# One place a turn for score items and conditioning rows, and two bank pairs for the channel tiles

## The chip, the cores and the metric

The kernel runs on one core of a Trainium2 chip. What is measured is the device time of one execution, in microseconds (us); smaller is better.

## What is computed

One layer of a decoder for 512 prompt tokens and 8 x 8 sample tokens, 576 in all, 1024 wide. The part that matters here is the first half of the layer:

```
mod = silu(c) @ w_ada + b_ada            # 6 x 1024 columns, 9 conditioning vectors
sh1, sc1, g1, sh2, sc2, g2 = split(mod, 6)
h = rmsnorm(x, norm_pre1) * (1 + sc1) + sh1
bg, cg, ua, q, k, v, r, lr, ga, gb = split(h @ w_in)
y_a = bg * causal_conv3(cg * ua)         # branch A, 1024 channels
scores = q k^T with decay, causal        # branch B, 4 heads, evaluated in blocks
merged = sigmoid(ga) * y_a + sigmoid(gb) * y_b
```

All inputs are float32. The large products are made of three passes over high and low parts (`hi*hi`, `hi*lo`, `lo*hi`).

## The kernel before

The program is written by hand as five instruction streams (TensorE, VectorE, ScalarE, GpSimd, SyncE) that wait for each other's semaphores. Each stream runs strictly in the order of its code.

The convolution stage is the loop `for j in range(KT)` in each stream, with eight turns, one for each 128 channels. In a turn TensorE makes four **channel tiles** with `channel_tile` (L1874): `cg`, `ua`, `bg` and `ga`, called tile 0 to tile 3 below. Each is 48 matmuls of 128x128 by 288 tokens into one pair of PSUM banks; there are four pairs, banks 0-1, 2-3, 4-5 and 6-7. Before the change the tiles go round the pairs 0, 1 and 2, so a tile waits until the one three tiles back has been taken out of PSUM. Who takes them out:

- tile 0: ScalarE copies it to `buf_a` (`cg_done`, L1024);
- tile 1: VectorE multiplies it by `buf_a` into `ext` (`u_done`, L1373, three pieces), then convolves `ext` (L519, L522);
- tile 2: VectorE multiplies it by the convolution (`t_done`, L1389);
- tile 3: ScalarE takes its sigmoid into `buf_b` (`sga_done`, L1042), and VectorE multiplies `y_a` by it (`ya_done`).

Three kinds of small work ride along on TensorE, all of them with a stationary operand only 32 columns wide:

- **Score items** (`score_item`, L1982). Turn j does level j of the block scores: five items in turn 0, three in turns 1 to 3, two in turns 4 to 7. Each is written to bank 7 and merged into `score` by VectorE (`take_item`, L581). Since all items share bank 7, each waits until the one before has been taken (`item_taken`).
- **Conditioning rows** (`ada_pair`, L2009). Two a turn, 4 matmuls of 512 columns each, into bank 6. The two together are one group of sums. VectorE copies them to `rows_ada` (L1411).
- **The way back** (`mod_back`, L1995). It turns the rows of the turn before round into bank 7, from where `take_mod` (L586) adds them to `mod`.

Where they stand is set by the variable `e` in TensorE's loop: even `e` is a channel tile, then come the items that `after_tile(j, e)` names; `ada_pair` stands at `e` = 3 and 7, `mod_back` at `e` = 6.

```
slots = (0, 2, 4, 6, 7) if j == 0 else (0, 2, 4)
```

On the other streams: ScalarE splits the weights (`high`, L931), GpSimd makes their low halves (`low`, L860), SyncE issues the loads in one fixed order (L667 for tiles, L680 for conditioning weights). The load of conditioning weights x waits for `ada_mm >= (x - 4) // 2 + 1`, and all loads behind it wait too. `qd_exp(j + 1)` on ScalarE waits until all items of level j have been made.

Of the kernel before, what the change touches and what calls it, by code (L numbers as in the profile page):

```python
# [39 lines left out]
KT = D // P  # L40
# [80 lines left out]
def layer_program(nc, a):  # L121
# [127 lines left out]
    def one_bank(b):  # L249
        return bank[b // 2][:, b % 2, :]  # L250
# [7 lines left out]
    def S(name):  # L258

        if name not in sems:  # L260
            sems[name] = nc.alloc_semaphore(name)
        return sems[name]
# [18 lines left out]
    def kc(tile):  # L281

        return tile[:, :].rearrange("p (k c) -> p k c", c=P)
# [31 lines left out]

    def c1_pair(j, i):

        return (4 * j + i) % 3

    ada_raw = [raw_c[i] for i in (0, 1, 4, 5)]  # L320

# [95 lines left out]
        items += [(lv, g) for g in ([[0], [1], [2], [3]] if B == 0 else [[0, 1], [2, 3]])]  # L417
        items += [(lv, [4])] if B < 8 else []

    def after_tile(j, e):  # L420

        level = [i for i, it in enumerate(items) if it[0] == j]
        slots = (0, 2, 4, 6, 7) if j == 0 else (0, 2, 4)
        return [i for i, slot in zip(level, slots) if slot == e]

    def items_to(lv):

        return sum(1 for it in items if it[0] <= lv)
# [135 lines left out]
    def take_item(dve, i):  # L564

        lv, chunks = items[i]
        B = LEVELS[lv]
        src = one_bank(7)
        ch, nch = chunks[0] * HEADS, len(chunks) * HEADS
        m = ROWS[chunks[0]]  # L570
        dve.wait_ge(S("item"), i + 1)
        if B == 0:
            dst = score[0:m, ch:ch + nch, 0:m]
            msk = ident[0:m, 0:m].bitcast(I32).rearrange("p (o t) -> p o t", o=1).to_broadcast([m, nch, m])
            data = src[0:m, 0:nch * m].rearrange("p (c t) -> p c t", t=m)
        else:
            dst = score[0:m, ch:ch + nch, 0:m].rearrange("p c (n s b) -> p c n s b", s=2, b=B)[:, :, :, 1, :]
            msk = mask[0:m, lv - 1, 0:m // 2].bitcast(I32).rearrange("p (o n b) -> p o n b", o=1, b=B) \
                .to_broadcast([m, nch, m // 2 // B, B])
            data = src[0:m, 0:nch * m // 2].rearrange("p (c n b) -> p c n b", c=nch, b=B)  # L580
        dve.copy_predicated(dst, msk, data).then_inc(S("item_taken"), 1)  # L581

    def take_mod(dve, j):
# [68 lines left out]
    with nc.Block() as block:  # L652
# [609 lines left out]
        def _(dve):  # L1262
# [96 lines left out]

            for j in range(KT):  # L1360
                n = TILE_C1 + 4 * j
                for i in after_tile(j, 0):
                    take_item(dve, i)

                if j > 0:
                    dve.wait_ge(S("tail_done"), 2 * j)
                    dve.wait_ge(S("conv"), 3 * j)
                hist = ext[:, S0E:EXT].rearrange("p (s w) -> p s w", w=TS + 2)[:, :, 0:2]
                dve.tensor_copy(hist, mix0[:, :, j].rearrange("p (s w) -> p s w", w=2)).then_inc(S("hist"), 1)
                dve.wait_ge(S("cg_done"), j + 1)  # L1370
                dve.wait_ge(S("ring_free"), n + 2)
                for src, dst, lo, hi in conv_pieces(c1_pair(j, 1), ext, 2, TS + 2, 2):
                    dve.tensor_tensor(dst, src, piece(buf_a, lo, hi), ALU.mult).then_inc(S("u_done"), 1)  # L1373
                for i in after_tile(j, 2):
                    take_item(dve, i)
                dve.wait_ge(S("u_done"), 3 * (j + 1))
                dve.wait_ge(S("hist"), j + 1)
                if j > 0:
                    dve.wait_ge(S("t_done"), 3 * j)
                conv(dve, ext, cv, [prm[:, CW + 8 * w + j:CW + 8 * w + j + 1] for w in range(3)],  # L1380
                     prm[:, CB + j:CB + j + 1], "conv", 3 * j)
                tails(dve, tail_mix[:, :, j], "tail_done")
                for i in after_tile(j, 4):
                    take_item(dve, i)
                dve.wait_ge(S("conv"), 3 * j + 3)

                dve.wait_ge(S("ring_free"), n + 3)
                for src, cvp, lo, hi in conv_pieces(c1_pair(j, 2), cv, 0, TS + 2, 2):
                    dve.tensor_tensor(piece(y_a[:, j, :], lo, hi), src, cvp, ALU.mult).then_inc(S("t_done"), 1)  # L1389
                if j + 1 < KT:  # L1390
                    dve_level(dve, j + 1)
                else:

                    dve.wait_ge(S("exps"), 1)
                    dve.tensor_tensor(k[:, :, :], k[:, :, :], suf[:, :, :], ALU.mult).then_inc(S("decayed"), 1)
                    dve.wait_ge(S("exps"), 2)
                    dve.tensor_tensor(q[:, :, :], q[:, :, :], pre[:, :, :], ALU.mult).then_inc(S("decayed"), 1)
                for i in after_tile(j, 6):
                    take_item(dve, i)
                if j > 0:  # L1400
                    take_mod(dve, j - 1)
                dve.wait_ge(S("t_done"), 3 * (j + 1))
                dve.wait_ge(S("sga_done"), j + 1)
                dve.tensor_tensor(y_a[:, j, :], y_a[:, j, :], buf_b[:, :], ALU.mult).then_inc(S("ya_done"), 1)
                for i in after_tile(j, 7):
                    take_item(dve, i)

                dve.wait_ge(S("ada_mm"), 2 * (j + 1))
                if j > 0:
                    dve.wait_ge(S("back"), j)  # L1410
                dve.tensor_copy(rows_ada[:, :], one_bank(6)[:, :]).then_inc(S("rows_ada"), 1)  # L1411

            take_mod(dve, KT - 1)
            dve.wait_ge(S("mod_done"), 9)
# [360 lines left out]
        def _(pe):  # L1775
# [176 lines left out]
            def score_item(i):  # L1952

                lv, chunks = items[i]
                B = LEVELS[lv]
                dst = one_bank(7)
                if B:
                    pe.wait_ge(S("qd_done"), lv)
                    if B > 1:
                        pe.wait_ge(S("kd_done"), lv - 1)  # L1960

                if i > 0:
                    pe.wait_ge(S("item_taken"), i)
                if lv >= 2:
                    pe.wait_ge(S("mod_done"), lv)
                kk = kd if B > 1 else k
                col = 0
                for c in chunks:
                    w = ROWS[c]
                    for h in range(HEADS):  # L1970
                        wide = max(B, 16) if B else 32
                        for g in range(w // 32):
                            key = 32 * g
                            if B == 0:
                                at_, rhs = key, q[:, h, P * c:P * c + w]
                            else:
                                if key % (2 * B) >= B > 16:
                                    continue
                                at_ = key // (2 * B) * B if B > 16 else key // 2
                                first = (h * T + P * c) // 2 if B < 8 else (h * SEQ + P * c) // 2  # L1980
                                rhs = qd[:, first:first + w // 2]
                            ins = pe.matmul(dst[key:key + 32, col + at_:col + at_ + wide],  # L1982
                                            kk[:, h, P * c + key:P * c + key + 32], rhs[:, at_:at_ + wide], start=True, stop=True)
                        col += w // 2 if B else w
                ins.then_inc(S("item"), 1)

            def mod_back(j):

                pe.wait_ge(S("rows_ada"), j + 1)
                pe.wait_ge(S("item_taken"), items_to(min(j + 1, KT - 1)))  # L1990
                if j > 0:
                    pe.wait_ge(S("mod_done"), j + 1)
                for m in range(4):
# [18 lines left out]

            pe.wait_ge(S("c_split"), 5)
            for j in range(KT):
                for e in range(8):
                    if e % 2 == 0:
                        n = TILE_C1 + 4 * j + e // 2
                        pe.wait_ge(S("w_lo_done"), n + 1)
                        if n < TILE_C1 + 2:
                            pe.wait_ge(S("v_summed"), n - TILE_C1 + 1)  # L2020
                        before = 4 * j + e // 2 - 3
                        if before >= 0:
                            name, count = (("cg_done", 1), ("u_done", 3), ("t_done", 3), ("sga_done", 1))[before % 4]
                            pe.wait_ge(S(name), count * (before // 4 + 1))
                        channel_tile(kc(w_hi[n % 4]), kc(w_lo[n % 4]), c1_pair(j, e // 2), (h_hi, h_lo))
                    elif e % 4 == 3:
                        ada_pair(2 * j + e // 4)
                    for i in after_tile(j, e):
                        score_item(i)
                    if e == 6 and j > 0:  # L2030
                        mod_back(j - 1)

            def tails_and_mod():

# [312 lines left out]
```

## Time and profile before

| | |
|---|---|
| median of 3 runs | 1012.21 us (1010.62 to 1012.27) |
| span of the profiled execution, first to last instruction | 1007.4 us |
| what lies around that span, against the median | 4.8 us |
| TensorE matmuls busy | 987.9 us, 98% of the span |
| VectorE, ScalarE, GpSimd busy | 543.0, 385.9, 228.6 us |

Busy time is the union of an engine's instructions. Matmuls overlap in their pipeline, so a busy TensorE can still do little work: how far apart two matmuls start says more than how long one lasts.

### The profile page before, as it was taken

The page shows a single profiled execution, that of the slowest core. Times are in us where ns is not written, and L with a number is a line of the kernel's source. Part 1 is how long each engine was busy: PE and PEld are TensorE (multiplying, and loading weights), DVE is VectorE, ACT ScalarE, POOL GpSimd, SP SyncE. Part 2 cuts the span into 40 slices and gives each one's busy share as a digit, 9 for nine tenths or more (in the row PEclk, how much of TensorE's full clock was granted, in tenths as well). Part 3 has the DMA queues.
Part 4 walks back from the last instruction along what each step waited for, and adds up shares of the span by engine and source line. Part 5 has one row for each costly group of instructions (what it writes and reads, how often), then busy time and mean ns, then how long its engine had stood idle before and what let it go on. Part 6 is the DMA issues. An engine that isn't in the chain of part 4 may idle for free.

```text
span 1007.4 us, 18705 instructions
## 1 busy us (share of the span) xinstructions
PE 987.9 (98%) x7743; PEld 897.7 (89%) x7743; DVE 543.0 (54%) x868; ACT 385.9 (38%) x588; POOL 228.6 (23%) x124
## 2 busy tenths in 40 slices
PE   7799999999999999999999999999999999999997
PEld 5689889999999999899998789999999999888886
DVE  2501104667555665346436688877777778750204
ACT  4532533143343334443463345333333334533212
POOL 2043433233343333233343020000000000013330
PEclk9999999999999999999999999999999999999999
DMA  9565344598366657545427042222322222323212
GB/s 354 171 93 180 116 90 96 129 115 136 106 193 165 138 128 139 91 105 160 123 91 219 1 124 86 64 85 84 85 84 85 84 85 63 126 64 100 79 59 94
DMA packets 144132, 115.59 MB, mean 115 GB/s; under 512 B 11353, under 2 KB 123761, under 8 KB 143025
## 3 DMA queue, kind: packets, MB, share of 16 engines
q1 hardware_dynamic: 143953, 114.38, 43.5%
q8 instruction: 61, 1.00, 0.4%
q14 instruction: 22, 0.18, 0.1%
q10 hardware_dynamic: 96, 0.04, 0.0%
HBM read 107.02 MB, written 7.35 MB: 114 GB/s over the span
## 4 chain that ended last, share of the span: by engine, by line
PE 93%; SPq 2%; DMA 1%; ACT 1%; DVE 1%; issue 1%; DVEq 0%
PE pair L1874 50%; PE pair L1929 16%; PE pair L2250 10%; PE pair L2203 5%; PE pair L2009 1%; PE pair L1982 1%; DMA raw<-in_w_in 1%; PE pair L1861 1%; SPq L667 1%; SPq L705 1%; PE pair L1921 1%; PE pair L2072 1%; PE pair L2061 1%; PE pair L1922 1%; PE pair L1923 1%
## 5 line engine op out<-in xcount | busy, mean ns | idle before, releaser
L1874 PE MATMUL pair<-h_hi,w_hi 128*128 128x288 f32 x1280 | 285.6, 301 | 0.1
L1874 PE MATMUL pair<-h_hi,w_lo 128*128 128x288 f32 x1280 | 279.1, 296 | 0.0
L1874 PE MATMUL pair<-h_lo,w_hi 128*128 128x288 f32 x1280 | 278.8, 295 | 0.0
L860 POOL TENSOR_TENSOR w_lo<-raw,w_hi 128x1024 fp32r<-128x1024 f32 x57 | 140.1, 2459 | 601.5 <-ACT w_hi L931 601.5
L1874 PEld LDWEIGHTS pair<-h_hi,w_hi 128*128 128x128 f32 x1280 | 207.2, 189 | 18.4 <-issue 16.3
L1874 PEld LDWEIGHTS pair<-h_lo,w_hi 128*128 128x128 f32 x1280 | 207.6, 188 | 0.0
L1874 PEld LDWEIGHTS pair<-h_hi,w_lo 128*128 128x128 f32 x1280 | 207.7, 188 | 0.0
L931 ACT ACTIVATE w_hi<-raw 128x1024 fp32r<-128x1024 f32 x70 | 73.5, 1056 | 160.5 <-PE pair L1923 75.7
L860 POOL TENSOR_TENSOR w_lo<-raw_c,w_hi 128x1024 fp32r<-128x1024 f32 x24 | 68.2, 2846 | 124.7 <-ACT w_hi L931 124.7
L1929 PE MATMUL pair<-w_hi,f_hi 128*128 128x512 f32 x176 | 68.9, 391 | 0.0
L1929 PE MATMUL pair<-w_lo,f_hi 128*128 128x512 f32 x176 | 68.7, 390 | 0.0
L1929 PE MATMUL pair<-w_hi,f_lo 128*128 128x512 f32 x176 | 68.5, 389 | 0.0
L1164 ACT ACTIVATE cv<-cv 128x592 f32<-128x592 f32 x22 | 15.4, 700 | 106.3 <-DVE cv L522 106.3
L2250 PE MATMUL pair<-t_hi,w_hi 128*128 128x288 f32 x144 | 42.5, 295 | 0.0
L2250 PE MATMUL pair<-t_lo,w_hi 128*128 128x288 f32 x144 | 42.5, 295 | 0.0
L2250 PE MATMUL pair<-t_hi,w_lo 128*128 128x288 f32 x144 | 42.4, 295 | 0.0
L1929 PEld LDWEIGHTS pair<-w_hi,f_lo 128*128 128x128 f32 x176 | 33.1, 188 | 7.0
L1929 PEld LDWEIGHTS pair<-w_hi,f_hi 128*128 128x128 f32 x176 | 33.0, 188 | 7.0
L1929 PEld LDWEIGHTS pair<-w_lo,f_hi 128*128 128x128 f32 x176 | 33.0, 188 | 6.8
L522 DVE SCALAR_TENSOR_TENSOR cv<-ext,ffp,cv 128x592 f32<-128x592 f32 x44 | 36.7, 834 | 1.6
L931 ACT ACTIVATE w_hi<-raw_c 128x1024 fp32r<-128x1024 f32 x24 | 25.2, 1055 | 26.8 <-PE pair L1874 12.0
L2250 PE MATMUL pair<-h_hi,w_hi 128*128 128x288 f32 x108 | 31.8, 294 | 0.0
(349 smaller groups left out, 1603.5 us busy)
## 6 DMA issues: line engine op xcount, KB each, us to landing
raw<-in_w_in SPq DMA_DIRECT2D x256, 64.0 KB, 3.1
raw_c<-in_w_ada SPq DMA_DIRECT2D x32, 512.0 KB, 5.8
raw_c<-in_w_in SPq DMA_DIRECT2D x192, 64.0 KB, 3.6
raw<-in_w_up SPq DMA_DIRECT2D x24, 512.0 KB, 4.7
raw<-in_w_down SPq DMA_DIRECT2D x22, 512.0 KB, 3.7
raw_up<-in_w_up SPq DMA_DIRECT2D x20, 512.0 KB, 3.8
ada_first<-in_w_ada SPq DMA_DIRECT2D x8, 1024.0 KB, 13.8
raw<-in_w_in SPq DMA_DIRECT2D x8, 512.0 KB, 4.7
```

The costliest lines, as they stand in the source:

```text
L522: dve.scalar_tensor_tensor(dst[:, :], src[:, tap:tap + CONV], w[tap], dst[:, :], ALU.mult, ALU.add) \
L667: sp.dma_start(dst[:, i, :], src[:, i, :]).then_inc(S(raw_name(n)), 16)
L705: sp.dma_start(ada_first[:, i, :], w_ada[P * i:P * i + P, 0:2 * D]).then_inc(S(f"ada_in{i}"), 16)
L860: pool.tensor_tensor(lo, raw_tile(n)[:, :], hi.bitcast(F32), ALU.subtract).then_inc(S("w_lo_done"), 1)
L931: act.activation(dst, raw_tile(n)[:, :], ACT.Copy).then_inc(S("w_hi_done"), 1)
L1164: act.activation(cv[:, :], cv[:, :], ACT.Gelu_apprx_tanh).then_inc(S("gelu_done"), 1)
L1861: ins = pe.matmul(bank[n][:, half, 0:HALF], w[:, i, :], x[:, i, HALF * half:HALF * half + HALF], start=i == 0 and p == 0, stop=i == KT - 1 ...
L1874: ins = pe.matmul(bank[pair][:, half, 0:HALF], w[:, i, :], x[:, i, HALF * half:HALF * half + HALF], start=i == 0 and p == 0, stop=i == KT ...
L1921: pe.matmul(dst[0:64, :], first_i[:, 0:64], wl[:, 0, :], start=False, stop=False)
L1929: ins = pe.matmul(one_bank(banks[t])[0:m, :], x, w[:, i, :], start=first and i == 0 and p == 0, stop=last and i == 1 and p == 2)
L2203: ins = pe.matmul(bank[wo_pair(x)][0:n, c, :], xx, w[:, 512 * c:512 * c + 512], start=y == 0 and p == 0, stop=y == KT - 1 and p == len(pas ...
L2250: ins = pe.matmul(dst, w[:, i, :], x[:, i, :], start=i == 0 and p == 0, stop=i == 3 and p == 2)
```

## The change

Every score item of a turn stands behind tile 1, and so do the way back and both conditioning pairs. Only turn 0 puts its last two items behind tile 3, since there are five. The items go to three banks (4, 5 and 7) in place of one; in bank 7 they stand at column 64, clear of the 36 columns of the way back. To free banks 4 and 5, the channel tiles alternate between pairs 0 and 1, so each now waits for the tile two back. VectorE takes the items after the tails of the convolution and copies `rows_ada` before the `t_done` products.

```
     def c1_pair(j, i):
-        return (4 * j + i) % 3
+        return (4 * j + i) % 2
...
-    def after_tile(j, e):
-        level = [i for i, it in enumerate(items) if it[0] == j]
-        slots = (0, 2, 4, 6, 7) if j == 0 else (0, 2, 4)
-        return [i for i, slot in zip(level, slots) if slot == e]
+    def after_tile(j, i):
+        level = [x for x, it in enumerate(items) if it[0] == j]
+        return level[:3] if i == 1 else level[3:] if i == 3 else []
+    def item_place(x):
+        lv = items[x][0]
+        slot = x - items_to(lv - 1)
+        return one_bank((4, 5, 7, 4, 5)[slot]), 64 if slot == 2 and lv > 0 else 0
...
                 tails(dve, tail_mix[:, :, j], "tail_done")
-                for i in after_tile(j, 4):
+                for i in after_tile(j, 1):
                     take_item(dve, i)
+                if j > 0:
+                    take_mod(dve, j - 1)
+                dve.wait_ge(S("ada_mm"), 2 * (j + 1))
+                if j > 0:
+                    dve.wait_ge(S("back"), j)
+                dve.tensor_copy(rows_ada[:, :], one_bank(6)[:, :]).then_inc(S("rows_ada"), 1)
                 dve.wait_ge(S("conv"), 3 * j + 3)
...
-                if i > 0:
-                    pe.wait_ge(S("item_taken"), i)
-                if lv >= 2:
-                    pe.wait_ge(S("mod_done"), lv)
+                if lv > 0:
+                    pe.wait_ge(S("item_taken"), items_to(lv - 1))
+                elif i > 2:
+                    pe.wait_ge(S("item_taken"), i - 2)
...
-                pe.wait_ge(S("item_taken"), items_to(min(j + 1, KT - 1)))
+                pe.wait_ge(S("item_taken"), items_to(j))
...
             for j in range(KT):
-                for e in range(8):
+                for i in range(4):
...
-                        before = 4 * j + e // 2 - 3
+                    before = 4 * j + i - 2
...
+                    if i == 1 and j > 0:
                         mod_back(j - 1)
+                    for x in after_tile(j, i):
+                        score_item(x)
+                    if i == 1:
+                        ada_pair(2 * j)
+                        ada_pair(2 * j + 1)
```

On TensorE, turn 1, the end of tile 1 and what follows it before the change (`raw_c_80` to `raw_c_85` are the four buffers of conditioning weights):

```order
L1982 MATMUL pair<-qd,k 32x16 [waits item_taken,qd_done]
L1982 MATMUL pair<-qd,k 32x16 x31
L2009 MATMUL pair<-raw_c_80,c_wide 32x512 [waits rows_ada,ada_raw_in1,ada_raw_in0]
```

The same place after the change (lines move by three: L1992 is the way back, L1979 a score item, L2006 a conditioning pair):

```order
L1992 MATMUL pair<-fold_all,rows_ada 32x9 [waits item_taken,rows_ada]
L1992 MATMUL pair<-fold_all,rows_ada 32x9 x15
L1979 MATMUL pair<-qd,k 32x16 [waits item_taken,qd_done]
L1979 MATMUL pair<-qd,k 32x16 x31
L1979 MATMUL pair<-qd,k 32x16 [waits item_taken,qd_done]
L1979 MATMUL pair<-qd,k 32x16 x31
L1979 MATMUL pair<-qd,k 32x16 [waits item_taken,qd_done]
L1979 MATMUL pair<-qd,k 32x16 x7
L2006 MATMUL pair<-raw_c_80,c_wide 32x512 [waits rows_ada,ada_raw_in1,ada_raw_in0]
L2006 MATMUL pair<-raw_c_80,c_wide 32x512
L2006 MATMUL pair<-raw_c_81,c_wide 32x512 x2
L2006 MATMUL pair<-raw_c_84,c_wide 32x512 [waits ada_raw_in3,ada_raw_in2]
```

One item and one pair became the way back, three items and both pairs. Behind tiles 0, 2 and 3 nothing small is left in this turn.

On VectorE, turn 1, from the products of tile 1 to those of tile 2, before:

```order
L1373 TENSOR_TENSOR ext<-pair,buf_a 128x8x8
L581 COPY_PREDICATED score<-mask,pair 128x512 [waits item]
L519 TENSOR_SCALAR cv<-ext,prm 128x592 [waits t_done,hist,u_done]
L522 SCALAR_TENSOR_TENSOR cv<-ext,prm,cv 128x592 [waits conv] x2
L527 COPY tail_mix<-ext 128x2
L529 COPY tail_mix<-ext 128x16
L581 COPY_PREDICATED score<-mask,pair 64x4x32 [waits item]
L1389 TENSOR_TENSOR y_a<-pair,cv 128x288 [waits ring_free,conv]
```

And after, with L586 as the taking of an item and L1391 as the copy to `rows_ada`:

```order
L1376 TENSOR_TENSOR ext<-pair,buf_a 128x8x8
L524 TENSOR_SCALAR cv<-ext,prm 128x592 [waits t_done,hist,u_done]
L527 SCALAR_TENSOR_TENSOR cv<-ext,prm,cv 128x592 [waits conv] x2
L532 COPY tail_mix<-ext 128x2
L534 COPY tail_mix<-ext 128x16
L586 COPY_PREDICATED score<-mask,pair 128x512 [waits item] x2
L586 COPY_PREDICATED score<-mask,pair 64x4x32 [waits item]
L591 TENSOR_TENSOR mod<-pair,prm 128x36 [waits back]
L1391 COPY rows_ada<-pair 128x512 [waits back,ada_mm]
L1396 TENSOR_TENSOR y_a<-pair,cv 128x288 [waits ring_free,conv]
```

Three items, the sum into `mod` and the copy to `rows_ada` now stand between the convolution and the products of tile 2.

## Rows read from the trace of the kernel before

**Rows 1.** Cores: span, mean granted TensorE clock.
```profile
core 0: 1007.4 us, clock 0.999
```

**Rows 2.** Chain that ended last, 140 to 420 us: start us, us, what.
```profile
151.59 6.40 PE pair L1874 x48
...
181.53 6.59 PE pair L1874 x48
...
272.36 6.58 PE pair L1874 x48
...
287.79 12.98 PE pair L1874 x96
...
331.70 6.58 PE pair L1874 x48
...
361.23 6.58 PE pair L1874 x48
...
391.53 3.38 PE pair L1874 x24
```

**Rows 3.** Timeline of TensorE, turn 1: start us, us, engine, line, tiles, shapes.
```profile
194.67 0.42 PE L1874 MATMUL pair<-h_lo,w_hi 128*128 128x288 f32 x2
194.93 0.43 PE L1874 MATMUL pair<-h_hi,w_lo 128*128 128x288 f32 x2
195.29 0.73 PE L1982 MATMUL pair<-qd,k 128*32 128x16 f32 x64
195.89 1.06 PE L2009 MATMUL pair<-raw_c,c_wide 128*32 128x512 f32 x8
196.89 0.53 PE L1874 MATMUL pair<-h_hi,w_hi 128*128 128x288 f32 x2
197.26 0.42 PE L1874 MATMUL pair<-h_lo,w_hi 128*128 128x288 f32 x2
...
203.46 0.43 PE L1982 MATMUL pair<-qd,k 128*32 128x16 f32 x16
...
210.40 0.44 PE L1995 MATMUL pair<-fold_all,rows_ada 128*32 128x9 f32 x32
210.68 1.07 PE L2009 MATMUL pair<-raw_c,c_wide 128*32 128x512 f32 x8
211.67 0.53 PE L1874 MATMUL pair<-h_hi,w_hi 128*128 128x288 f32 x2
```

**Rows 4.** Timeline of TensorE: an item of turns 0, 6 and 7.
```profile
179.75 0.46 PE L1982 MATMUL pair<-q,k 128*32 128x32 f32 x32
...
338.21 0.70 PE L1982 MATMUL pair<-qd,kd 128*32 128x32 f32 x32
...
367.74 1.09 PE L1982 MATMUL pair<-qd,kd 128*32 128x64 f32 x32
```

**Rows 5.** All matmuls of `ada_pair` (L2009): duration ns min/median/max, first and last start.
```profile
L2009 PE MATMUL pair<-raw_c,c_wide x128: 589/592/617, 165.2 to 390.9; 128*32 128x512 f32 x128
```

**Rows 6.** Timeline of VectorE, turn 2, from the products of tile 1.
```profile
225.75 0.89 DVE L1373 TENSOR_TENSOR ext<-pair,buf_a 128x288 f32<-128x288 f32 x3 [3.29 <-PE pair L1874]
226.56 1.32 DVE L581 COPY_PREDICATED score<-mask,pair 128x512 f32<-128x512 int32 x1
227.68 1.93 DVE L519 TENSOR_SCALAR cv<-ext,prm 128x592 f32<-128x592 f32 x1
229.64 1.70 DVE L522 SCALAR_TENSOR_TENSOR cv<-ext,prm,cv 128x592 f32<-128x592 f32 x2
```

**Rows 7.** Timeline of ScalarE, end of turn 3; brackets: idle before, releaser.
```profile
271.14 1.06 ACT L931 ACTIVATE w_hi<-raw_c 128x1024 fp32r<-128x1024 f32 x1 [2.39 <-DMA raw_c<-in_w_in]
...
273.51 0.66 ACT L1042 ACTIVATE buf_b<-pair 128x576 f32<-128x576 f32 x1
```

**Rows 8.** Windows of turn 2: us, busy of PE, PEld, DVE, ACT, POOL; PEclk, DMA share, GB/s.
```profile
212.00:242.00 30.00, 29.98 (x384) 27.56 (x382) 21.82 (x23) 10.44 (x10) 11.88 (x5) 1.00 0.99 121
```

**Rows 9.** Waits of SyncE's queue, 150 to 400 us: total us, times, longest.
```profile
SPq L680 <- PE pair L2009: 61.2, 10, 13.8
```

More of the change, by code:

```diff
@@ L567, in take_item @@
         B = LEVELS[lv]
-        src = one_bank(7)
+        src, at_ = item_place(i)
         ch, nch = chunks[0] * HEADS, len(chunks) * HEADS
@@ L574, in take_item @@
             msk = ident[0:m, 0:m].bitcast(I32).rearrange("p (o t) -> p o t", o=1).to_broadcast([m, nch, m])
-            data = src[0:m, 0:nch * m].rearrange("p (c t) -> p c t", t=m)
+            data = src[0:m, at_:at_ + nch * m].rearrange("p (c t) -> p c t", t=m)
         else:
@@ L579, in take_item @@
                 .to_broadcast([m, nch, m // 2 // B, B])
-            data = src[0:m, 0:nch * m // 2].rearrange("p (c n b) -> p c n b", c=nch, b=B)
+            data = src[0:m, at_:at_ + nch * m // 2].rearrange("p (c n b) -> p c n b", c=nch, b=B)
         dve.copy_predicated(dst, msk, data).then_inc(S("item_taken"), 1)
@@ L1361, in _ @@
                 n = TILE_C1 + 4 * j
-                for i in after_tile(j, 0):
-                    take_item(dve, i)
                 if j > 0:
@@ L1373, in _ @@
                     dve.tensor_tensor(dst, src, piece(buf_a, lo, hi), ALU.mult).then_inc(S("u_done"), 1)
-                for i in after_tile(j, 2):
-                    take_item(dve, i)
                 dve.wait_ge(S("u_done"), 3 * (j + 1))
@@ L1397, in _ @@
                     dve.tensor_tensor(q[:, :, :], q[:, :, :], pre[:, :, :], ALU.mult).then_inc(S("decayed"), 1)
[L1398 to L1401, printed above, removed]
                 dve.wait_ge(S("t_done"), 3 * (j + 1))
@@ L1404, in _ @@
                 dve.tensor_tensor(y_a[:, j, :], y_a[:, j, :], buf_b[:, :], ALU.mult).then_inc(S("ya_done"), 1)
-                for i in after_tile(j, 7):
+                for i in after_tile(j, 3):
                     take_item(dve, i)
[L1408 to L1411, printed above, removed]
             take_mod(dve, KT - 1)
@@ L1955, in score_item @@
                 B = LEVELS[lv]
-                dst = one_bank(7)
+                dst, col = item_place(i)
                 if B:
@@ L1960, in score_item @@
                         pe.wait_ge(S("kd_done"), lv - 1)
-                if i > 0:
-                    pe.wait_ge(S("item_taken"), i)
-                if lv >= 2:
-                    pe.wait_ge(S("mod_done"), lv)
+                if lv > 0:
+                    pe.wait_ge(S("item_taken"), items_to(lv - 1))
+                elif i > 2:
+                    pe.wait_ge(S("item_taken"), i - 2)
                 kk = kd if B > 1 else k
-                col = 0
                 for c in chunks:
@@ L2014, in _ @@
             for j in range(KT):
-                for e in range(8):
[L2016 to L2020, printed above, removed]
-                        before = 4 * j + e // 2 - 3
[L2022 to L2030, printed above, removed]
-                        mod_back(j - 1)
+                for i in range(4):
+                    n = TILE_C1 + 4 * j + i
+                    pe.wait_ge(S("w_lo_done"), n + 1)
+                    if n < TILE_C1 + 2:
+                        pe.wait_ge(S("v_summed"), n - TILE_C1 + 1)
+                    before = 4 * j + i - 2
+                    if before >= 0:
+                        name, count = (("cg_done", 1), ("u_done", 3), ("t_done", 3), ("sga_done", 1))[before % 4]
+                        pe.wait_ge(S(name), count * (before // 4 + 1))
+                    channel_tile(kc(w_hi[n % 4]), kc(w_lo[n % 4]), c1_pair(j, i), (h_hi, h_lo))
+                    if i == 1 and j > 0:
+                        mod_back(j - 1)
+                    for x in after_tile(j, i):
[3 more added lines that the diff above has]
+                        ada_pair(2 * j + 1)
             def tails_and_mod():
```

## The prediction

> **What bounds the kernel now.** I read the chain of work that ended last first. From 151.59 us to 391.53 us it consists of TensorE matmuls and nothing else long enough to be listed, turn after turn [rows 2]. So in the convolution stage TensorE sets the time, and what an engine beside it gains or loses counts only if TensorE has to wait for it. The granted clock is 0.999 over the whole span [rows 1] and 1.00 in the stage [rows 8], the higher level of 2.4 GHz, so a matmul costs the same everywhere.
>
> Next I asked how much of the stage is the small work. A channel tile that follows large matmuls takes 6.40 us (the first row of [rows 2]). Where tiles 2 and 3 follow each other the two take 12.98, which is 2 x 6.40 and 0.18 for the small work around them. The stage runs for 391.53 - 151.59 = 239.94 us, and its 32 tiles need 32 x 6.40 = 204.80. The other **35.14 us** are small work and the switches into and out of it. By turns [rows 2]: turn 0 has 29.94 - 25.60 = 4.34, turns 1 to 3 have 90.83 - 76.80 = 14.03, turns 4 and 5 have 59.34 - 51.20 = 8.14, turn 6 has 3.93, turn 7 has 4.70.
>
> Then I took such a place apart with TensorE's timeline [rows 3]. Pairs of large matmuls start 0.26 to 0.27 apart (194.67, 194.93). The first small one starts 0.36 after the last pair: **entering** costs 0.09. The item lasts 0.60 until the conditioning pair starts, and that one 1.00 until the tile starts. The tile's first pair then takes 0.37 (196.89 to 197.26): **leaving** costs 0.10. The largest piece is in the 1.00. A conditioning matmul lasts 0.59 [rows 5] and the eight recorded ones of a pair cover 1.06, so the last starts some 0.48 after the first, and the tile can't start until that last one is nearly through. Since work of the same 32-column shape needn't wait for that (the pair at 195.89 starts while the item's 0.73 still run), the end of a place costs more than its middle. That is what the change can save.
>
> **The change, part by part.**
>
> *Fewer places.* Before, turn 0 has 4 places, turns 1 to 3 have 4 and turns 4 to 7 have 3: 28 in all. After, there is one a turn and a second in turn 0: 9. The matmuls are the same in number and shape, so I price each new place by what stands in it.
>
> - entering 0.09, leaving 0.10 [rows 3];
> - the way back 0.28 until the next small work (210.40 to 210.68);
> - a 64-matmul item 0.60; a 32-matmul item of turn 0 0.28 (its busy 0.46, like the way back's 0.44 [rows 3, 4]); the 16-matmul item 0.15 inside a place, at the 64-matmul item's rate of 9.4 ns, and 0.40 just before a tile (busy 0.43 [rows 3]);
> - an item of turn 6 0.54 and of turn 7 0.93, their busy 0.70 and 1.09 [rows 4] less the 0.16 that overlaps in the way back;
> - the last conditioning pair 1.00 until the tile [rows 3];
> - the first conditioning pair until the second: no row shows it. Eight recorded matmuls on four strips of 32 columns are two rounds. The second round starts before 0.48, so a round is about 0.44 and the pair 0.88. From below it is 0.48, if the second pair's first round starts as soon as the first pair's last matmul has started; from above 1.00, if every pair is waited for as a tile waits. I take 0.88, since no change of shape lies between the two.
>
> Turn 0: 0.09 + 3 x 0.28 + 0.88 + 1.00 + 0.10 = 2.91, and behind tile 3 0.09 + 0.28 + 0.40 + 0.10 = 0.87, together 3.78. Turns 1 to 3: 0.09 + 0.28 + 2 x 0.60 + 0.15 + 0.88 + 1.00 + 0.10 = 3.70 each, 11.10. Turns 4 and 5 without the short item: 3.55 each, 7.10. Turn 6: 3.43. Turn 7: 4.21. The sum is **29.62**, so the stage gets 35.14 - 29.62 = 5.52 shorter, and the first tile behind it loses its 0.10 of leaving: **5.6 us**.
>
> On the second pair the Trainium skill says otherwise. "TensorE: Matmul & The Clock Gate", section "Back-to-back issue gap", gives N/2.4 + 2.5 ns between matmuls at the full clock, 216 ns for 512 columns, where the rows need about 440. With its figure the second pair would cost 0.43 in place of 0.88, and the gain would be an estimated 9.2 us. The trace's own two rounds in 1.06 don't agree with it for these float32 operands.
>
> *Three banks for the items.* The wait of an item for the one before goes. It costs little now, since it lay under other work; I count nothing.
>
> *Two bank pairs for the tiles.* A tile now waits for the one two back, so whoever takes a tile out of PSUM has one tile's time, 6.40 us. Tile 0 of the next turn waits for VectorE's `t_done`. Counted from the end of tile 1, VectorE needs 0.81 for the products, 1.96 and 1.70 for the convolution, at most 3 x 1.12 for the three items [rows 6] and, for two tails, the sum into `mod` and the copy to `rows_ada`, which I bound by one more 1.93: 9.8 us. Tile 2 ends 3.6 + 6.4 = 10.0 us after tile 1, so its products start on time, take about 0.9, and the next turn's tile 0 is 5.5 us further on. What hides the moved work is tile 2 itself. The level work that follows on VectorE moves a little earlier than now, since it doesn't wait for an item behind tile 2. ScalarE's `qd_exp` moves from behind tile 2 to behind tile 1, which is only earlier.
>
> *Loads.* SyncE stands 61.2 us waiting for conditioning pairs [rows 9]. The second pair of a turn now ends some 13 us earlier, so these loads and the tiles' loads behind them are issued earlier. The first pair ends about 2 us later than now behind tile 1 (way back and items stand ahead of it), and one tile's load behind it does too.
>
> **The rivals.**
>
> *ScalarE too late for two pairs.* In turn 3 a high half waited 2.39 us for its transfer, and the sigmoid of tile 3 ended at 274.17 [rows 7]. That tile ended about 1.4 us before turn 4 began at 272.36, at 270.9, so it was 3.2 us late. Before, nobody felt it, since the pair was wanted two tiles later. Now tile 1 of the next turn wants it after 6.4. By then TensorE is ahead by 4.34 + 14.03 - 3.78 - 11.10 = 3.5 us, and if the transfer doesn't come earlier the sigmoid is 6.7 late: a stall of 0.3. With transfers as crowded as in turn 2 (busy share 0.99 at only 121 GB/s [rows 8]) it could be 3 us in one or two turns. Time 1009 or so. For it: that stretch. Against: SyncE issues earlier.
>
> *The transfers set the pace, and nothing changes.* If the weights come at a fixed rate in the crowded stretch, TensorE meets the end of its lead and gives the 5.6 back: 1012.2. The crowded stretch speaks for it; against it, SyncE's 61.2 us of waiting for TensorE and a chain without one DMA in it [rows 2].
>
> *The second pair slips in.* At the lower bound of 0.48 the gain is 8 x 0.40 = 3.2 more: 1003.4.
>
> *Slower: VectorE can't empty tile 2 in time.* Items, `mod` and the copy now stand ahead of `t_done` in VectorE's strict order. TensorE stalls at tile 0 of every next turn once this chain runs more than 5.5 us over my 10.9, and loses the whole gain at 0.8 us more (5.6 over seven turns). At 9 us over it would be 3.5 x 7 = 24.5 lost, time 1031. Against it: my 9.8 holds the slow 1.96 already.
>
> *Slower: the clock falls.* If stalls at the tiles let TensorE's granted clock drop to the level of 1.2 GHz, a tile takes 12.8 and one turn costs 25.6 us more, time 1032. The rows show 1.00 and no wait to start it. The Trainium skill has such a case, in "TensorE: Matmul & The Clock Gate", section "A second HAM failure mode: psum-queue depth-cycling": short idle times while going round the PSUM banks made the clock swing.
>
> **How the numbers follow.** The profiled execution has a span of 1007.4 [rows 1], and 4.8 us lie around it up to the median of 1012.21. Neither is touched, so the span becomes 1001.8 and the time 1012.2 - 5.6 = **1006.6**. The bounds: the second pair gives 3.2 more or 1.0 less; if an item that is followed by an item costs its whole busy time (0.13 to 0.16 more, about 15 times), 2.2 less. So 1003.4 to 1009.8 by unknown costs alone, and 1003.2 to 1010.1 with a part of the first rival. The measurement tells 0.2%, 2 us, from no change. Chances: forecast 68%, second pair slips in 8%, ScalarE late 10%, transfers 7%, VectorE late 5%, clock 2%. Faster is the first three, 86%; same 7%; slower 7%.
>
> **What would show it.** Tile 0 of turns 0 and 1 should start about 29.4 us apart (29.94 now), then 29.3 in turns 1 to 3 (30.28), 29.15 in turns 4 and 5. From tile 1's last pair to tile 2's first there should be 3.5 to 3.9 us, with a pair to pair distance near 0.88. Tiles 0 and 1, and 2 and 3, should run through with no step. VectorE's `t_done` products should start right at the end of tile 2, `buf_b` before tile 0 is over. I am wrong if a place costs 5 us or more, if TensorE idles ahead of a tile 0 or 1 for `t_done` or `sga_done`, or if the stage is shorter and the end of the kernel isn't.

## The result, and the profile after

The changed kernel takes 1025.39 us (median of 4 runs, 1024.31 to 1027.98) against 1011.42 us before in the same comparison: ratio 1.014, 95% interval 1.0126 to 1.0154. It is slower by 14 us, where I had forecast 5.6 us faster, and it lies outside my range of 1003.2 to 1010.1.

The span of its profiled execution is 1022.6 us, 15.2 more than [rows 1]. Its chain of work that ended last answers to [rows 2] (start us, us, what; L1872 is a channel tile, L1992 the way back, L1979 an item, L2006 a conditioning pair):

```profile
152.41 12.80 PE pair L1872 x96
...
194.59 0.37 PE pair L1992 x32
194.96 1.09 PE pair L1979 x83
196.05 1.82 issue
197.87 0.55 PE pair L1979 x23
198.42 1.76 PE pair L2006 x14
200.19 25.78 PE pair L1872 x192
...
227.40 5.18 issue
232.57 0.77 PE pair L1979 x29
233.34 3.49 PE pair L2006 x11
236.84 26.41 PE pair L1872 x192
...
264.62 6.41 issue
271.04 0.79 PE pair L1979 x29
...
271.88 3.44 PE pair L2006 x14
275.32 26.00 PE pair L1872 x192
...
331.87 1.43 issue
...
393.96 16.18 PE pair L1872 x120
```

The pieces called "issue" are new in the stage: TensorE stands still and waits for nothing that the profile shows, no semaphore and no tile. There are four, in turns 1, 2, 3 and 5, and their sum is 1.82 + 5.18 + 6.41 + 1.43 = 14.84 us. The list of TensorE's waits in the stage holds nothing else (engine, line, waited for, total us, times, longest):

```profile
PE pair L1979 <- issue: 14.8, 4, 6.4
```

TensorE's timeline shows where one falls, in the place that answers to [rows 3]:

```profile
194.52 0.44 PE L1992 MATMUL pair<-fold_all,rows_ada 128*32 128x9 f32 x32
194.79 1.26 PE L1979 MATMUL pair<-qd,k 128*32 128x16 f32 x119
197.87 0.55 PE L1979 MATMUL pair<-qd,k 128*32 128x16 f32 x24 [1.82 <-issue]
```

A small float32 matmul of the program is two matmuls in the trace, each with a weight load of its own, so the items of this turn have 64, 64 and 16 matmuls. The stop comes 119 recorded matmuls into them, inside the second, where no instruction waits for anything.

These windows answer to [rows 8] (us, busy of PE, PEld, DVE, ACT, POOL; PEclk, DMA share, GB/s):

```profile
212.00:242.00 30.00, 24.82 (x331) 21.70 (x330) 16.01 (x18) 8.71 (x8) 7.36 (x3) 0.89 0.82 119
...
223.00:230.00 7.00, 4.40 (x169) 4.13 (x167) 3.85 (x5) 1.06 (x1) 3.26 (x2) 1.00 1.00 64
230.00:236.00 6.00, 3.43 (x46) 1.34 (x46) 4.26 (x8) 2.51 (x3) 0.00 (x0) 0.61 0.07 13
```

After the two long stops the granted clock falls; behind the first it is 0.61 on average over 230 to 236 us. The conditioning pairs behind them last 3.49 and 3.44 us instead of 1.76: twice as long, the level of 1.2 GHz. With the tiles behind (26.41 and 26.00 instead of 25.78) and the rests of the items that makes 4.7 us.

The stage runs from 152.41 to 393.96 + 12.80 = 406.76, so 254.35 us, 14.41 more than the 239.94 of before. That is my 5.5 saved, 14.84 stopped, 4.7 at the low clock, and 0.4 that I do not attribute.

**What TensorE stops for.** The page of the changed kernel has a queue that I had passed over (queue, kind: packets, MB, share of 16 engines):

```profile
PE 987.9 (97%) x7743; PEld 900.3 (88%) x7743; DVE 547.8 (54%) x868; ACT 385.5 (38%) x588; POOL 229.3 (22%) x124
...
q8 instruction: 61, 1.00, 0.4%
```

7743 matmuls, 7743 weight loads and, by my count of the program, 261 others (semaphores and the like) are 15,747 instructions on TensorE. 61 packets of 16 KB brought them, so one packet holds some 258 instructions; the distance of the stops, below, makes it 256. ("Packet" means such a packet of instructions from here on; the pieces of the weight loads are called rows.) I counted the program's instructions up to each stop, and took from the trace when a packet of that queue was moved:

```
turn  stop at instruction   packet starts   TensorE goes on
1     3010                  195.65          197.87
2     3778                  230.39          232.57
3     4546                  268.72          271.04
5     6082                  330.75          333.30
```

The stops are 3, 3 and 6 times 256 instructions apart, and TensorE goes on 2.2 to 2.6 us after the start of a packet. It ran out of instructions. In the tiles 256 instructions are 128 large matmuls and last 17 us. In the new place they are used in about 1.2 us, an estimate from the price list of the prediction. A place of turns 1 to 3 holds 389 of them, so a packet can begin and end inside one place. Before, no place holds more than 145.

What else the DMA engines did at the four stops (turns 1, 3 and 5 here, turn 2 above at 223 to 230 us):

```profile
192.00:198.00 6.00, 4.18 (x180) 3.91 (x179) 3.23 (x5) 1.06 (x1) 2.47 (x2) 1.00 0.01 3
259.00:268.00 9.00, 5.62 (x173) 5.36 (x172) 3.91 (x9) 1.06 (x1) 3.32 (x2) 1.00 0.23 62
328.00:334.00 6.00, 4.57 (x187) 4.04 (x189) 3.38 (x5) 1.36 (x2) 2.47 (x2) 1.00 0.01 3
```

In turns 1 and 5 they moved next to nothing, and yet TensorE stopped for 1.82 and 1.43 us: a packet that nothing disturbs is already too slow for a place that uses one up in 1.2 us. In turns 2 and 3, with the stops of 5.18 and 6.41 us, the 512-byte rows of the tile loads were coming in: from 222 to 230 us and from 260 to 272 us every recorded piece of a load has 512 bytes (beside some of 4), about 120 of them a microsecond, 64 and 62 GB/s. The busy share is not the common sign, since it is 1.00 in turn 2, where one row takes 147 to 156 ns in the median until 228 us, and 0.23 in turn 3, where one takes 25. In turn 2 the packet was moved at 230.39, just when the stream of rows ended; in turn 3 it was moved at 268.72, while the stream ran until 272.

The Trainium skill knows these packets: "Runtime: NRT & Kernel Launch", section "Instruction fetch mechanics", has blocks of 16 KiB with 256 instructions, fetched over a DMA queue of the sequencer's own while the current one runs. It calls this "mostly hidden", since instructions leave more slowly than blocks arrive. The size agrees with the trace. The second part doesn't hold here: 14.84 us weren't hidden.

### The profile page after: what moved, and what is told of

Its sections match the earlier page's. It is cut to its first block, busy times and chain, and to the rows that moved or that the text cites. A ratio compares the mean times of both kernels' runs of the same rounds, so it can differ in the third digit from the quotient of the medians.

```text
span 1022.6 us, 18691 instructions
## 1 busy us (share of the span) xinstructions
PE 987.9 (97%) x7743; PEld 900.3 (88%) x7743; DVE 547.8 (54%) x868; ACT 385.5 (38%) x588; POOL 229.3 (22%) x124
## 4 chain that ended last, share of the span: by engine, by line
PE 92%; SPq 2%; issue 2%; DMA 1%; ACT 1%; DVE 1%; DVEq 0%
PE pair L1872 49%; PE pair L1927 16%; PE pair L2247 10%; PE pair L2200 5%; PE pair L2006 2%; PE pair L1979 1%; DMA raw<-in_w_in 1%; PE pair L1859 1%; SPq L672 1%; SPq L710 1%; PE pair L1919 1%; PE pair L2069 1%; PE pair L2058 1%; PE pair L1920 1%; PE pair L1921 1%
## 5 line engine op out<-in xcount | busy, mean ns | idle before, releaser
L1872 PE MATMUL pair<-h_hi,w_hi 128*128 128x288 f32 x1280 | 284.2, 300 | 0.1
L1872 PE MATMUL pair<-h_hi,w_lo 128*128 128x288 f32 x1280 | 279.3, 296 | 0.0
L1872 PE MATMUL pair<-h_lo,w_hi 128*128 128x288 f32 x1280 | 279.2, 296 | 0.0
L1872 PEld LDWEIGHTS pair<-h_hi,w_hi 128*128 128x128 f32 x1280 | 208.1, 189 | 13.7 <-issue 12.1
L1872 PEld LDWEIGHTS pair<-h_lo,w_hi 128*128 128x128 f32 x1280 | 208.0, 189 | 0.0
L1872 PEld LDWEIGHTS pair<-h_hi,w_lo 128*128 128x128 f32 x1280 | 208.0, 189 | 0.0
L1376 DVE TENSOR_TENSOR ext<-pair,buf_a 128x288 f32<-128x288 f32 (+2 forms) x24 | 7.1, 351 | 63.8 <-PE pair L1872 63.8
```

The lines of the kernel that those rows point to most:

```text
L1872: ins = pe.matmul(bank[pair][:, half, 0:HALF], w[:, i, :], x[:, i, HALF * half:HALF * half + HALF], start=i == 0 and p == 0, stop=i == KT ...
```

## The experiments

Ratios are to the kernel before in the same comparison, with 95% intervals. "Stops" are the issue pieces of the chain within the stage, those under 0.1 us left out. In all kernels, the one before too, three more lie outside it, about 0.94, 2.86 and 1.16 us, and are left out. The times are medians, but the stops are those of the one execution that was profiled, and they vary from one to the next. Where that execution lies far from the median, its time is given.

**1. The two bank pairs alone**, in the kernel before, with all small work in its old places:

```
-            return (4 * j + i) % 3
+            return (4 * j + i) % 2
-                        before = 4 * j + e // 2 - 3
+                        before = 4 * j + e // 2 - 2
```

> The kernel before with one part of the change alone: channel tiles alternate between two bank pairs and wait for the tile two back; small work stays in its old 28 places, items one after the other in bank 7. Theory 1 (instruction supply: a place holds up to 389 TensorE instructions that run in some 3 us, and the next packet of 256 comes late): no change, 1010.5 to 1012.5 us, no stall. Theory 2 (two pairs are too few, TensorE waits for whoever empties a tile): most of the loss is here already, 1016 us or more.

Measured: 1011.1 us, ratio 1.0004 (0.9994 to 1.0013), with one stop of 0.17. The bank pairs cost nothing that can be measured. The loss comes with the places.

**2. Where the packets end.** Tiny matmuls (9 columns into bank 5, nobody reads the result) ahead of turn 0 move the ends of the packets against the program: 28 of them are 112 instructions (56 matmuls and 56 weight loads more in the trace), 12 are 48, and 64 are 256, one whole packet, which moves nothing.

```
             keep_warm(16)
+            for x in range(28):
+                g = x % 4
+                pe.matmul(one_bank(5)[32 * g:32 * g + 32, 0:9], ident[:, 32 * g:32 * g + 32], ident[:, 0:9],
+                          start=True, stop=True)
```

> The changed kernel with 28 tiny float32 matmuls (112 TensorE instructions, about 0.5 us) long before the stage, which only move every later instruction by 112 against the packets of 256. Theory 1: packet ends move from 48, 38, 28, 18, 41 instructions into the places of turns 1 to 5 to 192, 182, 172, 162, 185, with the one before in the tile ahead, so the packet has 4 us more to come: the idle pieces (14.8 us) and the slow clock after them go, 1006 to 1009 us. Theory 2 and theory 3 (three items in a row wait for VectorE in some way the profile does not name): nothing moves, 1025 us.

> Control for the run before it: 64 tiny matmuls, 256 instructions, one whole packet, at the same place. Theory 1: the packet ends fall on the same instructions of the stage as in the changed kernel, so it stays slow, 1023 to 1028 us, with idle pieces in turns 1, 2, 3 and 5 at the same instructions. If it is as fast as with 112, the extra work or the later start helps, and not where the packets end.

> As the run with 28 tiny matmuls, but 12 of them, 48 instructions. Theory 1, now with a price: in the changed kernel the time from the request to the arrival of a packet was about 3.9 us in turns 1 and 5 and 8 to 10 us in the crowded turns 2 and 3. A shift of 48 asks some 3 us earlier (48 instructions of a tile), so turns 1 and 5 lose their idle pieces, turns 2 and 3 keep about 2 and 3 us of theirs, with some slow clock: 1009 to 1015 us, between the shifts 0 and 112. Theory 3 (semaphores between items): 1025 us.

| instructions added | time, us | ratio | stops, us |
|---|---|---|---|
| 0 (the changed kernel) | 1025.39 | 1.014 (1.0126 to 1.0154) | 1.82, 5.18, 6.41, 1.43 |
| 48 | 1012.35 | 1.0005 (0.999 to 1.0019) | 2.65, 1.32 |
| 112 | 1009.75 | 0.9992 (0.9975 to 1.0009) | 2.69 |
| 256 | 1022.19 | 1.011 (1.0093 to 1.0127) | 2.15, 0.80, 8.12, 0.34, 1.43 |

Adding work that does nothing makes the kernel 13 to 16 us faster, unless it is one whole packet; then most of the loss is back. That is hard to explain by anything but the packets' ends. The details are off: with 112 I had expected no stop and at most 1009 us, and with 256 at least 1023 us and none of the 0.34 in turn 4. The profiled execution took 1009.47 us with 48 and 1011.54 with 112. With 112 instructions more, the one stop that is left has moved. The chain of that kernel, turn 3 (seen up to 285 us):

```profile
258.06 1.76 PE pair L2010 x14
259.82 2.71 PE pair L1876 x19
262.54 2.69 issue
265.22 19.78 PE pair L1876 x135
```

It stands 19 matmuls into tile 2 now, in the midst of plain large matmuls, where the next packet begins by the count. The granted clock fell behind this stop too, to 0.77 over 262.5 to 270 us.

**3. Two places a turn** instead of one:

```
-                    if i == 1 and j > 0:
+                    if i == 0 and j > 0:
                         mod_back(j - 1)
-                    for x in after_tile(j, i):
+                    placed = after_tile(j, 1)
+                    if n == TILE_C1:
+                        pe.wait_ge(S("v_summed"), 2)
+                    for x in placed[:1] if i == 0 else placed[1:] if i == 1 else after_tile(j, i):
                         score_item(x)
```

> The changed kernel with two places a turn in place of one: the way back and the first item behind tile 0, the other items and both conditioning pairs behind tile 1 (193 and 195 instructions in turns 1 to 3). Two bank pairs and three item banks stay. Theory 1: in any stretch of 256 instructions at least 61 belong to a tile (4 us), so idle pieces are gone or under 1 us; eight more places at 0.28 us each cost 2.2 us of the 5.6: 1008 us (1006.5 to 1011). Theory 2: as slow as the changed kernel, 1020 us or more, since the pairs are the same. Theory 3: better in part, since items 1 and 2 still follow each other.

Measured: 1008.82 us, ratio 0.998 (0.9967 to 0.9993), one stop of 1.04 in turn 2. By the same price list and my count of where the packets end, a packet that lies over the places now lasts 7.4 us or more in turns 1 to 5, in place of 1.2. Most of the change is kept here (three banks, two pairs, both conditioning pairs together), and it beats both kernels.

**4. The same one place, but the conditioning pairs between the first item and the second**, so that slow matmuls stand amid the fast ones:

```
                     placed = after_tile(j, i)
                     for x in placed[:1]:
                         score_item(x)
                     if i == 1:
                         ada_pair(2 * j)
                         ada_pair(2 * j + 1)
+                    for x in placed[1:]:
+                        score_item(x)
```

> The changed kernel with both conditioning pairs moved between the first and the second item of a place. Same instructions, same number of places, packet ends at the same counts; but the 33 slow instructions of the pairs (1.8 us) now lie between the request and the use of a packet, in turns 1 to 5. Theory 1: every idle piece is about 1.7 us shorter: turns 1 and 5 none, turns 2 and 3 about 3.5 and 4.5 us, time 1014 to 1020 us. Theory 3: items 2 and 3 start 1.8 us later as well, so it could gain the same in turns 1 and 5, but the idle pieces would stand at an item's start and not 194 instructions past a multiple of 256.

Measured: 1013.06 us, ratio 1.0009 (0.9986 to 1.0031), a little under the 1014 that I had expected at least. The ten runs go from 1008.64 to 1017.55, and the profiled one is the slowest. It has stops of 3.53 and 6.04 in turns 2 and 3 and none in turns 1 and 5. 1.8 us more between asking and using remove the small stops; the large ones they shorten by 1.65 and 0.37 here. So the packets come later in turns 2 and 3 than in 1 and 5.

**5. Without the conditioning loads** (28 of 32, 512 KB each; later turns multiply the first weights again). The same in the kernel before is the control.

```
                 if x >= 4:
-                    sp.wait_ge(S("ada_mm"), (x - 4) // 2 + 1)
+                    return
```

> The changed kernel without the conditioning loads past the first four (28 loads of 512 KB in the stage are left out, and TensorE uses the first four again). Theory 1 with crowding as its second part: a packet then comes in about 3.9 us everywhere, so the idle pieces of turns 2 and 3 shrink from 5.2 and 6.4 us to 1.2 and 0.6, those of turns 1 and 5 stay near 1.8 and 1.4, and the clock does not fall: 1009 to 1013 us. If the pieces stay as long, other transfers have nothing to do with it.

> The kernel before without the same loads, for comparison with the run before it. It has no idle pieces in the stage, so nothing changes by more than 1 us: 1010 to 1012 us. The changed kernel without these loads should then lie within 2 us of it: 5.6 us gained by fewer places, about 5 us of idle pieces left.

Measured: 1026.86 us, ratio 1.0152 (1.0135 to 1.0169), stops of 4.44, 4.75, 3.27 and 2.26 in turns 1, 2, 3 and 5, in sum 14.7. The control: 1012.24, ratio 1.001 (1.0 to 1.0019), with stops of 1.14 and 0.38. My expectation was wrong: the packets are late without the conditioning loads too. The edit does a second thing, though: SyncE no longer waits in front of these loads, so the tile loads behind them are issued earlier and fall on other turns. In turn 1 the DMA engines' share over 192 to 198 us is now 0.79 with 51 GB/s, instead of 0.01 with 3, the packet is moved 3.48 us after the place begins instead of 1.06, and the stop has grown from 1.82 to 4.44. The lateness goes with the tile loads, in 512-byte rows.

**6. Long rows for the tile loads.** Each 64 KB load of the stage reads 16 rows of 4 KB instead of 128 of 512 bytes; these kernels multiply other weights. Again with the kernel before as control.

```
                     for i in range(KT):
+                        if TILE_C1 <= n < TILE_C2:
+                            r = P * (n % KT) + 16 * i
+                            sp.dma_start(raw_tile(n)[16 * i:16 * i + 16, :], w_in[r:r + 16, 0:1024]) \
+                              .then_inc(S(raw_name(n)), 16)
+                            continue
                         sp.dma_start(dst[:, i, :], src[:, i, :]).then_inc(S(raw_name(n)), 16)
```

> The changed kernel, with the loads of the stage's 32 tiles reading 16 whole rows of w_in (4 KB in one piece) in place of 128 rows of 512 bytes. Bytes, number of transfers and order on SyncE are the same; the weights that are multiplied are other ones, so this part of the result is another computation. Theory (TensorE's next packet of instructions waits behind a backlog of small packets of the tile loads): the packets of instructions arrive some 3.9 us after they are asked in turns 2 and 3 too, as they do in turns 1 and 5. The idle pieces of the chain shrink from 5.2 and 6.4 us there to 1 to 2, all of them together to 4 to 6 us, the granted clock stays at 1.00, and the time is 1009 to 1014 us. Rival (the packet size of the loads has nothing to do with it): 1025 as before.

> Control for the run with long rows: the kernel before with the same edit of the tile loads. Both theories: no idle piece in the stage, 1010 to 1012.5 us. If it becomes faster than 1009, the loads did bind the kernel before, and the other run has to be read against this one.

Measured: 1010.78 us, ratio 0.9998 (0.9985 to 1.0011), and the control 1010.68, ratio 0.9993 (0.9982 to 1.0004). So the edit is worth nothing in the kernel before and over 14 us in the changed one, which still has none of the 5.6 us that I had forecast. The chain with long rows:

```profile
153.06 12.80 PE pair L1877 x96
...
196.42 2.24 issue
...
228.18 1.35 issue
...
259.02 0.31 issue
...
261.69 25.80 PE pair L1877 x192
...
290.83 25.78 PE pair L1877 x192
...
318.03 1.34 issue
...
380.01 16.18 PE pair L1877 x120
```

The stops are 5.24 us in all, none is over 2.3, and the granted clock stays at 1.00 through the stage. Where the difference lies is told by the time at which the move of a place's packet starts, counted from the start of the place (us, from the same queue of the traces as above):

| turn | short rows: place, packet, difference | long rows: place, packet, difference |
|---|---|---|
| 1 | 194.59, 195.65, 1.06 | 194.94, 195.80, 0.86 |
| 2 | 225.97, 230.39, 4.42 | 226.75, 226.69, -0.06 |
| 3 | 263.25, 268.72, 5.47 | 257.63, 256.99, -0.64 |
| 4 | 301.32, 300.00, -1.32 | 287.48, 286.10, -1.38 |
| 5 | 330.44, 330.75, 0.31 | 316.61, 316.85, 0.24 |

In the quiet turns 1, 4 and 5 the packet comes at the same point of the program with either rows, within 0.2 us. In turns 2 and 3 it comes 4.5 and 6.1 us earlier with the long ones. Turn 4 has no stop in either kernel; its packet comes 1.3 us before the place begins, earlier than any other. The same 7 us that were full before the stop of turn 2 are now empty:

```profile
223.00:230.00 7.00, 5.65 (x209) 5.39 (x211) 3.07 (x5) 1.06 (x1) 3.47 (x2) 1.00 0.01 2
```

And the DMA issues from 212 to 302 us (line, times, KB, median us to landing), first with short rows in the changed kernel, then with long ones:

```profile
raw<-in_w_in SPq DMA_DIRECT2D x40, 64.0 KB, 6.3
raw_c<-in_w_in SPq DMA_DIRECT2D x40, 64.0 KB, 7.4
```

```profile
raw<-in_w_in SPq DMA_DIRECT2D x51, 64.0 KB, 3.6
raw_c<-in_w_in SPq DMA_DIRECT2D x48, 64.0 KB, 3.2
```

**7. Places laid out by the count.** First, two places a turn in turns 1 to 5 and one in turns 0, 6 and 7, whose places hold 228 instructions at most. Second, two places in turns 1 to 3 only, with 20 tiny matmuls ahead (80 instructions).

```
+                    two = 1 <= j <= 5
-                    if i == 1 and j > 0:
+                    if i == (0 if two else 1) and j > 0:
                         mod_back(j - 1)
-                    for x in after_tile(j, i):
+                    placed = after_tile(j, 1)
+                    for x in (placed[:1] if i == 0 else placed[1:] if i == 1 else []) if two else after_tile(j, i):
```

> The changed kernel with two places a turn in turns 1 to 5 (way back and first item behind tile 0, the other items and both pairs behind tile 1) and one place in turns 0, 6 and 7. Theory: no place of turns 1 to 5 uses up its instructions within 7.4 us of asking for the next packet, by the count, so no idle piece in the chain; the saving is that of the two-place kernel plus some 0.5 us for the two turns less with two places: 1006 to 1008.5 us. Rival (the gain of a place was never there): 1011.

> Two places in turns 1 to 3 only, one in all others, and 20 tiny matmuls (80 instructions) ahead of the first turn, which by the count puts the ends of the packets so that at least 7.4 us lie between asking and using in turns 1 to 3, and 5.1 and 3.6 in turns 4 and 5, where packets came in 4 us. Theory: no idle piece over 0.5 us; 1005.5 to 1008.5 us. Rival (the place of the packet's end does not matter, the two-place layout does): the same as the run with two places in turns 1 to 5, give or take 0.7.

Measured: 1005.36 us (6 runs), ratio 0.9943 (0.9929 to 0.9957), no stop at all. It is the fastest kernel of the study, and a little under my 1006 to 1008.5. The second: 1007.1 us, ratio 0.996 (0.9947 to 0.9974), with a stop of 1.23 in turn 2, where I had expected none over 0.5. The count gave it 7.4 us there, as it gave the first and the two-place kernel (stop of 1.04); why only the first got through without one, I can't say. The two kernels differ by 1.7 us. In their profiles the stage is 1.34 us longer in the second: 1.23 is the stop, 0.3 a wait for conditioning weights in turn 4, and two places less give some of it back. The chain of the first has nothing but TensorE in it:

```profile
153.33 12.80 PE pair L1872 x96
...
218.64 0.37 PE pair L1992 x32
219.00 0.58 PE pair L1979 x40
219.59 6.57 PE pair L1872 x48
226.16 1.04 PE pair L1979 x72
227.20 1.76 PE pair L2006 x14
228.96 19.38 PE pair L1872 x144
...
375.96 16.18 PE pair L1872 x120
```

## Why the prediction was wrong

**The step that failed** is in "Fewer places": "The matmuls are the same in number and shape, so I price each new place by what stands in it." That takes for granted that TensorE's instructions are there when it wants them. 389 instructions in 3.7 us need a new packet within 1.2 us, and in turns 1, 2, 3 and 5 it came 1.4 to 6.4 us too late. The supply of instructions is a term that the sum didn't have: it measured 14.84 us of stops and, behind them, 4.7 us at the low clock, against 5.5 saved. That is shown from two sides. Moving the packets' ends took away nearly all of the loss, and a whole packet brought most of it back; earlier delivery by long rows took 9.6 us of stops and the low clock away with the places unchanged. The lateness has two parts. In turns 1 and 5, with the DMA engines idle, a packet is 1.4 to 1.8 us too slow for such a place, and long rows change nothing there. In turns 2 and 3 the 512-byte rows add 4.5 and 6.1 us, by the table of experiment 6. What stays open is the way between: where a packet stands while the rows go ahead, and what sets their low rate. It isn't that the engines are always full, since their share was 0.23 in turn 3. No record tells when a packet is asked for.

**The prices were right.** With long rows the stage is 392.81 - 153.06 = 239.75 us. Less 5.24 of stops that is 234.51, and less the tiles' 204.80 it is 29.71 of small work, where I had 29.62. In the same chain the step from tile 2 of turn 3 to tile 2 of turn 4, without a stop, is 290.83 - 261.69 = 29.14, against my 29.15. The two conditioning pairs together cost 1.76 against my 0.88 + 1.00 = 1.88. So "the second pair slips in" didn't come true, nor did the 216 ns for 512 columns of the Trainium skill, "TensorE: Matmul & The Clock Gate", section "Back-to-back issue gap", which has this formula for a matmul by itself. In the kernel laid out by the count the stage is 388.76 - 153.33 = 235.43, which is 234.51 and 0.92 for the 5 more places, 0.18 each. It gives 4.5 us in the stage, and 5.7 were measured (interval 4.3 to 7.2): the gain was there to be had.

**VectorE late, ScalarE late: neither.** VectorE's timeline in turn 1 of the changed kernel, which answers to [rows 6]:

```profile
194.70 0.89 DVE L1376 TENSOR_TENSOR ext<-pair,buf_a 128x288 f32<-128x288 f32 x3 [9.60 <-PE pair L1872]
...
202.66 0.68 DVE L1391 COPY rows_ada<-pair 128x512 f32<-128x512 f32 x1
206.88 0.89 DVE L1396 TENSOR_TENSOR y_a<-pair,cv 128x288 f32<-128x288 f32 x3 [3.54 <-PE pair L1872]
```

The copy ends 8.6 us after tile 1 did, inside my 9.8, and VectorE then idles 3.54 us until tile 2 is there. In no kernel does the chain wait for ScalarE or VectorE within the stage. Experiment 1 says the same of the two pairs as a whole.

**Transfers.** I had them as a rival that gives the gain back by late weights. They did harm by another way: while their short rows come in, instructions come late. [rows 8] with 0.99 busy at 121 GB/s was a sign of it for turn 2, which I read only for what it does to weights; turn 3 had no such share (0.23 at 62 GB/s).

**The clock.** I gave it 2% and tied it to waits at the tiles. It did fall, but as a consequence of the stops, and cost 4.7 us in two turns, not 25.6 in one.

**Chances.** 7% for slower was too little. All my rivals that cost time began with waits that semaphores show. None was of the kind that has no line in the program.

## What to carry to other kernels

When many short instructions are gathered in one place, count instructions per microsecond as well as time: here TensorE gets 256 at a time, and 128 matmuls of 16 columns with their weight loads use them up in 1.2 us, too fast even for a packet that nothing disturbs. A kernel whose stops move when tiny work is added ahead, and come back with one packet's worth, is short of instructions; spreading the short work over two places left 1.04 us of stops or none here, and reading weights in longer rows 5.24 of 14.84. Look for "issue" pieces in the chain, and before packing work into one place for stretches in which the DMA queues move many short rows at a low rate, whatever the engines' busy share.

## What I had not expected of the hardware

- An idle TensorE in the middle of unconditional matmuls, for up to 8.12 us, because a 16 KB packet of instructions was late; for 1.82 and 1.43 us even with the DMA engines idle.
- A stream of 512-byte rows ran at 62 to 64 GB/s in two stretches, with the DMA engines' busy share at 1.00 in one and 0.23 in the other, and the same loads of 64 KB in 4 KB rows land in 3.2 to 3.6 us instead of 6.3 to 7.4. In the kernel before this has no price.
- After a stop of 5.18 us in an otherwise full stage the granted clock fell to the lower level, so that the next 3.5 us of work took twice as long. The length of the stop alone doesn't tell: after one of 2.15 (256 instructions added) the two pairs took 3.03 us instead of 1.76, after 2.24 (long rows) and 2.65 (48 added) they took 1.76 and 1.80.
